# TensorE's code for each expert split in two parts, with all first parts placed behind the comparisons

## The chip, the cores and the metric

The kernel runs on one core of one Trainium2 chip. The metric is the time of one execution on the device, in microseconds (us). The trace comes from one profiled execution of the kernel before. Engines are named PE (TensorE matmuls), PEld (TensorE weight loads), DVE (VectorE), ACT (ScalarE), POOL (GpSimd) and SP (SyncE, which here only issues transfers).

## The reference, cut to what matters

Two layers of an encoder trunk on 256 tokens of width 1024, in float32. The change touches only the last block, a top-2-of-8 mixture of experts. Each token goes to two experts; an expert is a SwiGLU of inner width 3584:

```python
def swiglu(u, wg, wu, wd):
    return (jax.nn.silu(u @ wg) * (u @ wu)) @ wd

logits = (t @ w_router).astype(jnp.float32) + b_router.astype(jnp.float32)
top_val, top_idx = lax.top_k(logits, TOP_K)
gates = jax.nn.softmax(top_val, axis=-1)
# every expert e: swiglu of its own tokens with w_gate_e[e], w_up_e[e], w_down_e[e]
# y[token] += gate * output, for both experts of the token
```

How many tokens an expert gets is known only when the program runs.

## The kernel before, in words

After the mixer layers and the dense block, the tokens are sorted by expert into `xs`. The eight experts then run one after the other. POOL copies the tokens of the next expert into `xe` (which lies in `mixT`), and signals `xe_ready`.

The inner width is cut into 14 stages of 256 columns. A stage has three units of 1 MB: two halves of gate and up weights ("gu", s, 0) and ("gu", s, 1), each with 4 of the 8 slices of the input width, and one unit of down weights. SP streams the 42 units of each expert in order into 14 slots; a slot is refilled when the product that read it has signalled (`last_use` in the SP program: `gu_full` for gate and up, `down_done` for down). So the transfers run up to 14 units ahead, and past the end of an expert into the next.

PE, ACT and DVE each hold the code of an expert in six variants, for at most 32, 64, 128, 160, 192 and 256 tokens. `experts` (line 631) writes the code of one engine: the block "next" counts the expert up, "pick" loads its number of tokens into a register, and the chain beginning at "tree" compares it with the bounds, one comparison to a bound, and jumps to the variant. The chain ends in `first_variant`, whose code lies right behind it; the other variants follow in order of size. For all three engines that is 128. Each variant ends in a jump to "next", announced by a hint at the variant's beginning (`mark_branch_hint_location`).

PE's variants, with the lines of the profile:

- 32 and 64 tokens (`expert_whole`, line 1359): gate and up as full float32 products with the tokens as the stationary side (L1370), each run as two matmuls and two weight loads: 64 matmuls in a stage for 32 tokens, 32 for 64 tokens. Then the turned activations (L1356) and the down product (L1382). The order is gate_up(0); gate_up(1), turn(0); gate_up(2), turn(1), down(0); and so on. gate_up(2) and turn(0) wait for `act_ready`, which DVE gives (L2374) behind ACT's silu.
- 160 and 192 (`expert_wide`, line 1401): stage 0 runs in full float32 over four banks, PG and TRB (`gate_up_whole`, L1411, 64 matmuls, the first 32 from unit 0). All later stages use weights and tokens split into two float32r parts (L1427 and L1433 gate and up, L1446 and L1455 down). ACT makes the upper part of a unit (an activation, shown at L1575) and DVE the lower (L2380). With `HI` = 3 buffers for upper parts, ACT's second conversion waits for `hi_used`, which PE signals in the products of unit 0. DVE takes the tokens apart (L2407, and L2413 in two halves, the first behind `hi_used`), then empties the banks of stage 0 (L2427); the second stage on PE waits for that.
- 128 and 256 (`expert_split`, line 1482): split products in all stages (L1492 gate and up, L1523 down), so that the first product waits for ACT's first conversion.

In this run the experts 0 to 7 take the variants 32, 32, 128, 64, 160, 32, 192 and 64.

The order of the beginning of an expert on PE before the change is one piece of code:

```python
def expert(e, n):
    pe.wait_ge(xe_ready, e + 1)
    (expert_whole if n < P else expert_split if n % P == 0 else expert_wide)(e, n)
```

Of the kernel before, what the change touches and what calls it, by code (L numbers as in the profile page):

```python
# [24 lines left out]
P = 128  # L25
# [19 lines left out]
EARLY = SLOTS - D // SW  # L45
USES = 3 * STAGES
# [242 lines left out]
def build(nc, ap, out, ypairs):  # L289
# [13 lines left out]
    with ExitStack() as ctx:  # L303
# [327 lines left out]
        def experts(eng, name, emit, first_variant=128):  # L631
# [19 lines left out]
            for at, n, then in zip([label("tree")] + after, tests, after):  # L651
                with nc.body(at, valid_engines=own):
                    if n < first_variant:
                        eng.br_lt(rows, n + 1, on_true=label(n), on_false=then)
                    else:
                        eng.br_lt(rows, NVAR[NVAR.index(n) - 1] + 1, on_true=then, on_false=label(n))
            for n in sorted(NVAR, key=lambda n: n != first_variant):
                with nc.body(label(n), valid_engines=own):
# [136 lines left out]
        def _(pe):  # L795
# [563 lines left out]
            def expert_whole(e, n):  # L1359
# [26 lines left out]
                for i in range(STAGES + 2):  # L1386
                    if i < STAGES:
                        gate_up(i)
                    if 1 <= i <= STAGES:
# [11 lines left out]
            def expert_wide(e, n):  # L1401
# [3 lines left out]
                def gate_up_whole():  # L1405

                    for h in range(2):
                        w = landed_unit(e, "gu", 0, h).rearrange("p (k g f c) -> p k f g c", k=KD // 2, g=2, f=2)
                        for i, bank in enumerate(banks):
                            for k in range(KD // 2):  # L1410
                                last = mm(bank[:, 0:n], w[:, k, i // 2, i % 2, :], xe[:, h * KD // 2 + k, 0:n],  # L1411
                                          start=(h == 0 and k == 0), stop=(h == 1 and k == KD // 2 - 1))
                            if i == 2:
                                used = last
                        (used if h else last).then_inc(hi_used, 1)
                    last.then_inc(gu_full, 2)
# [52 lines left out]
                gate_up_whole()  # L1469
# [12 lines left out]
            def expert_split(e, n):  # L1482
# [57 lines left out]

                for s in range(STAGES + 1):
                    if s < STAGES:
# [7 lines left out]
            def expert(e, n):  # L1550
                pe.wait_ge(xe_ready, e + 1)
                (expert_whole if n < P else expert_split if n % P == 0 else expert_wide)(e, n)

            experts(pe, "pe", expert)
# [1068 lines left out]
```

## Time and profile before

| | |
|---|---|
| median of 3 runs | 1706.28 us (1705.0 to 1706.72) |
| the profiled execution, its own time | 1703.9 us |
| its span in the trace | 1702.1 us |
| PE busy | 1511.3 us, 89% of the span |
| PEld, DVE, ACT, POOL busy | 1199.1, 723.3, 552.1, 63.1 us |
| chain that ended last | PE 79%, DMA 11%, issue 4%, DVE 3% |
| granted TensorE clock, mean | 0.955 of full speed |
| the eight experts | from about 706 to 1675 us of the span |

"Issue" is time in which an engine waited for nothing that the profile shows: no semaphore of another engine came late. Behind such a wait can stand a transfer, the engine's own sequencer, or the loading of its code. In the rows of a timeline the columns are start (us), length (us), engine, line, operation, out<-in with shapes, count, and in brackets the idle time of the engine just before and what ended it. For a matmul the first shape is the stationary side. The clock in tenths or as a fraction is of full speed: 1.0 is 2.4 GHz and 0.5 is 1.2 GHz.

### The profile page before, as it was taken

How to read it: one execution, taken by the hardware profiler on the slowest of the kernel's cores; microseconds unless marked ns; L12 is line 12 of the kernel's file. 1: busy time of each engine (PE TensorE's matmuls, PEld its weight loads, DVE VectorE, ACT ScalarE, POOL GpSimd, SP SyncE). 2: the span in 40 equal slices, each digit the busy share in tenths (PEclk: the TensorE clock that was granted, in tenths of full speed). 3: DMA queues.
4: the chain of work that ended last, by engine and by line, in shares of the span. 5: the costliest groups of instructions: out<-in, count | busy, mean ns of one | idle time of the engine just before them, and what ended most of it. 6: DMA issues, size and time to landing. Idle time of an engine off the chain costs nothing.

```text
span 1702.1 us, 29831 instructions
## 1 busy us (share of the span) xinstructions
PE 1511.3 (89%) x12054; PEld 1199.1 (70%) x12055; DVE 723.3 (42%) x1056; ACT 552.1 (32%) x769; POOL 63.1 (4%) x66
## 2 busy tenths in 40 slices
PE   5999999999999999865658999999997579999894
PEld 3867878999976776644546875579986468888452
DVE  2253265656534532400017881156762036665212
ACT  2134144444322421200007761046551025554101
POOL 0010000000010001000000000000000000000002
PEclk9999999999999999987788999999999889999998
DMA  9725566545442435699999999997577997555893
GB/s 352 276 92 238 205 249 272 198 173 198 159 168 99 174 149 221 273 423 423 425 425 426 416 391 401 426 422 291 235 284 304 424 423 289 223 223 223 318 425 149
DMA packets 74557, 488.85 MB, mean 287 GB/s; under 512 B 9792, under 2 KB 13920, under 8 KB 16544
## 3 DMA queue, kind: packets, MB, share of 16 engines
q1 hardware_dynamic: 72176, 479.94, 70.2%
q10 hardware_dynamic: 1648, 4.59, 0.8%
q8 instruction: 114, 1.87, 0.4%
q0 software_dynamic: 576, 2.10, 0.4%
q14 instruction: 43, 0.35, 0.1%
HBM read 482.66 MB, written 3.93 MB: 286 GB/s over the span
## 4 chain that ended last, share of the span: by engine, by line
PE 79%; DMA 11%; issue 4%; DVE 3%; ACT 1%; POOL 1%; SPq 1%; ACTq 0%; POOLq 0%; DVEq 0%
PE PG L1370 9%; PE PG L923 6%; PE Y L949 5%; DMA arena<-in_experts 5%; PE PG L1492 5%; PE PG L1427 4%; PE Y L1382 4%; PE Y L1455 4%; DMA ring<-in_experts 4%; PE TRB L1427 4%; PE Y L1211 3%; PE Y L957 3%; PE PG L925 3%; PE TRB L1433 3%; PE PG L1433 3%
## 5 line engine op out<-in xcount | busy, mean ns | idle before, releaser
L1370 PE MATMUL PG<-ring,mixT 128*32 128x128 f32 (+1 forms) x1920 | 119.8, 356 | 60.7 <-issue 56.1
L2396 DVE COPY arena<-TRB 128x64 f32<-128x64 f32 (+1 forms) x70 | 17.6, 251 | 340.7 <-PE TRB L1356 340.7
L1370 PEld LDWEIGHTS PG<-ring,mixT 128*32 128x32 f32 (+1 forms) x1920 | 92.0, 140 | 91.3 <-issue 76.6
L1575 ACT ACTIVATE parts<-ring 128x2048 fp32r<-128x2048 f32 x82 | 153.6, 1901 | 3.6 <-PE PG L1492 3.6
L923 PE MATMUL PG<-h_parts,parts 128*128 128x512 f32 x432 | 152.8, 394 | 1.4 <-DVE arena L2275 1.4
L1575 ACT ACTIVATE rope<-PG 64x128 f32<-64x128 f32 (+2 forms) x84 | 27.1, 323 | 377.5 <-PE PG L1370 353.9
L1370 PE MATMUL PG<-arena,mixT 128*32 128x128 f32 (+1 forms) x1664 | 101.8, 351 | 41.0 <-issue 41.0
L1370 PEld LDWEIGHTS PG<-arena,mixT 128*32 128x32 f32 (+1 forms) x1664 | 78.9, 139 | 68.8 <-issue 55.2
L925 PE MATMUL PG<-h_parts,parts 128*128 128x256 f32 x432 | 121.8, 282 | 0.0
L2260 DVE TENSOR_TENSOR parts<-ring,parts 128x2048 fp32r<-128x2048 f32 x42 | 95.1, 2290 | 32.7 <-ACT parts L1575 32.7
L2380 DVE TENSOR_TENSOR ring_parts<-ring,parts 128x2048 fp32r<-128x2048 f32 x40 | 90.6, 2288 | 31.7 <-PE Y L1446 16.3
L2380 DVE TENSOR_TENSOR parts<-arena,parts 128x2048 fp32r<-128x2048 f32 x42 | 95.2, 2288 | 17.7 <-PE Y L1446 15.1
L923 PEld LDWEIGHTS PG<-h_parts,parts 128*128 128x128 f32 x432 | 81.2, 188 | 19.4 <-DVE arena L2275 1.6
L949 PE MATMUL Y<-hT,ring 128*128 128x256 f32 x416 | 93.2, 384 | 0.0
L949 PEld LDWEIGHTS Y<-hT,ring 128*128 128x128 f32 x416 | 79.5, 193 | 11.5 <-issue 0.8
L925 PEld LDWEIGHTS PG<-h_parts,parts 128*128 128x128 f32 x432 | 81.3, 188 | 0.0
L1575 ACT ACTIVATE parts<-arena 128x2048 fp32r<-128x2048 f32 x42 | 78.9, 1901 | 3.6 <-PE PG L1492 3.6
L890 PE MATMUL Y<-parts 128*128 128x256 f32 x224 | 63.4, 283 | 0.2 <-DVE parts L2284 0.2
L892 PE MATMUL Y<-parts 128*128 128x256 f32 x224 | 63.4, 283 | 0.0
L891 PE MATMUL Y<-parts 128*128 128x256 f32 x224 | 63.4, 283 | 0.0
L957 PE MATMUL Y<-ring,hT 128*128 128x256 f32 (+2 forms) x320 | 57.3, 338 | 2.8 <-ACT hT L1575 2.8
L2380 DVE TENSOR_TENSOR parts<-arena,scr_parts 128x2048 fp32r<-128x2048 f32 x21 | 48.1, 2293 | 26.4 <-ACT scr_parts L1575 26.4
(364 smaller groups left out, 2675.1 us busy)
## 6 DMA issues: line engine op xcount, KB each, us to landing
ring<-in_experts SPq DMA_DIRECT2D x168, 1024.0 KB, 13.6
arena<-in_experts SPq DMA_DIRECT2D x168, 1024.0 KB, 16.9
ring<-in_weights SPq DMA_DIRECT2D x116, 1024.0 KB, 6.4
ring<-in_weights SPq DMA_DIRECT2D x4, 512.0 KB, 4.1
ypairs<-hT ACTq DMA_DIRECT2D x3, 512.0 KB, 6.6
tok<-in_x SPq DMA_DIRECT2D x1, 1024.0 KB, 9.0
result<-scr SPq DMA_DIRECT2D x2, 512.0 KB, 2.6
ring<-in_weights SPq DMA_DIRECT2D x2, 432.0 KB, 6.3
```

Of the source, the lines that this page charges most:

```text
L923: mm(PG[:, m, :].rearrange("p (i t) -> p i t", i=2), w_hi[d % SPLITS][:, c], h_parts[:, :, k, :], start=(k == 0), stop=False, skip_group_c ...
L925: last = mm(PG[:, m, 0:T], w_lo[d % SPLITS][:, c], h_hi[:, k, :], start=False, stop=(k == KD - 1), skip_group_check=True)
L949: last = mm(bank_part, ring[:, s, k, c:c + m], hT[:, k, :], start=(k == 0), stop=(k == KD - 1))
L957: last = mm(bank_part, hT[:, k, b * P:(b + 1) * P], ring[:, s, k, 0:m], start=(k == 0), stop=(k == KD - 1))
L1370: last = mm(bank[i * n:(i + 1) * n, 0:width], xe[:, k, 0:n], w[k // 4][:, k % 4, i * width:(i + 1) * width], start=(k == 0), stop=(k == KD ...
L1382: last = mm(o, actT[:, s % 2, f, 0:n], w[:, f, c:c + width], start=(s == 0 and f == 0), stop=(s == STAGES - 1 and f == 1))
L1427: last = mm(both, hi[:, k, i // 2, i % 2, :], h_parts[:, :, h * KD // 2 + k, 0:n], start=(h == 0 and k == 0), stop=False, skip_group_check ...
L1433: last = mm(bank[:, 0:n], lo[:, k, i // 2, i % 2, :], h_parts[:, 0, h * KD // 2 + k, 0:n], start=False, stop=(h == 1 and k == KD // 2 - 1) ...
L1492: last = mm(bank, x[j][:, h * KD // 2 + k, :], w[:, k, :], start=(opens and k == 0), stop=(closes and k == KD // 2 - 1))
L1575: return nc.scalar.activation(out_, in_, func, **kw)
L2260: V.tensor_tensor(w_lo[d % SPLITS], ring[:, slot_of[slot_of_dense(d)], :, :].rearrange("p k c -> p (k c)"), w_hi[d % SPLITS].bitcast(F32), ...
L2380: V.tensor_tensor(w_lo_e[q % SLOTS_E], ring_e[q % SLOTS_E].rearrange("p k c -> p (k c)"), w_hi_e[q % HI].bitcast(F32), ALU.subtract).then_ ...
```

## The change

PE's variants alone are cut in two. The first part ("head") has the wait for `xe_ready` and the first products: gate_up(0) for 32, 64, 128 and 256 tokens, and the half of stage 0 that reads unit 0 for 160 and 192. All six heads stand right behind the comparisons, in the order of `HEADS`; then come the rests, that of 64 first and then 32, 128, 160, 192, 256. A head ends in a jump to its rest, with a hint at the head's beginning. The chain of comparisons of PE now ends in 64 instead of 128. The products, their order in a variant and all semaphores stay; ACT's and DVE's code stays.

```diff
+HEADS = (64, 192, 160, 128, 32, 256)
...
-        def experts(eng, name, emit, first_variant=128):
+        def experts(eng, name, emit, first_variant=128, heads=None):
...
+            if heads:
+                for n in HEADS:
+                    with nc.body(label(n), valid_engines=own):
+                        on = eng.mark_branch_hint_location()
+                        heads(eng.snap(turn, min_val=0, max_val=NE - 1), n)
+                        eng.br(label(f"rest_{n}")).branch_hint(on)
             for n in sorted(NVAR, key=lambda n: n != first_variant):
-                with nc.body(label(n), valid_engines=own):
+                with nc.body(label(f"rest_{n}" if heads else n), valid_engines=own):
                     back = eng.mark_branch_hint_location()
                     emit(eng.snap(turn, min_val=0, max_val=NE - 1), n)
                     eng.br(label("next")).branch_hint(back)
...
-            def expert_whole(e, n):
+            def expert_whole(e, n, head):
...
-                for i in range(STAGES + 2):
+                if head:
+                    gate_up(0)
+                    return
+                for i in range(1, STAGES + 2):
...
-            def expert_wide(e, n):
+            def expert_wide(e, n, head):
...
-                gate_up_whole()
+                if head:
+                    gate_up_whole(0)
+                    return
+                gate_up_whole(1)
...
-            def expert_split(e, n):
+            def expert_split(e, n, head):
...
+                if head:
+                    gate_up(0)
+                    return
                 for s in range(STAGES + 1):
-                    if s < STAGES:
+                    if 0 < s < STAGES:
                         gate_up(s)
...
-            def expert(e, n):
+            def part(e, n, head):
+                (expert_whole if n < P else expert_split if n % P == 0 else expert_wide)(e, n, head)
+
+            def expert_head(e, n):
                 pe.wait_ge(xe_ready, e + 1)
-                (expert_whole if n < P else expert_split if n % P == 0 else expert_wide)(e, n)
-
-            experts(pe, "pe", expert)
+                part(e, n, True)
+
+            def expert_rest(e, n):
+                part(e, n, False)
+
+            experts(pe, "pe", expert_rest, first_variant=HEADS[0], heads=expert_head)
```

## Rows read from the trace of the kernel before

**Rows 1.** Windows: experts 1, 3 and 6; length, busy (x count), PEclk, DMA share, GB/s.

```profile
785.00:891.00 106.00, 65.50 (x1148) 49.58 (x1148) 8.47 (x32) 6.14 (x19) 1.90 (x1) 0.77 1.01 424
...
1023.00:1110.00 87.00, 84.47 (x619) 47.73 (x617) 10.77 (x29) 7.13 (x16) 1.90 (x1) 1.00 1.01 414
...
1375.00:1583.00 208.00, 198.79 (x1175) 169.92 (x1176) 122.23 (x101) 100.16 (x98) 1.90 (x1) 0.98 0.67 269
```

**Rows 2.** DMA queues, 784 to 797.5 us: packets, MB, share of 16 engines.

```profile
q8 instruction: 3, 0.05, 1.7%
```

**Rows 3.** Timeline of PE, start of expert 1 (32 tokens, behind an expert of 32).

```profile
791.54 2.79 PE L1370 MATMUL PG<-ring,mixT 128*32 128x128 f32 x48 [6.88 <-issue]
796.77 3.70 PE L1370 MATMUL PG<-ring,mixT 128*32 128x128 f32 x80 [2.44 <-issue]
```

**Rows 4.** Timeline of PE, start of expert 2 (128 tokens).

```profile
897.27 3.77 PE L1492 MATMUL PG<-scr_parts,h_parts 128*128 128x512 f32 x8 [6.98 <-ACT scr_parts L1575]
```

**Rows 5.** Timeline of PE, start of expert 3 (64 tokens, behind 128).

```profile
1023.50 2.38 PE L1370 MATMUL PG<-ring,mixT 128*64 128x256 f32 x20
1027.64 4.97 PE L1370 MATMUL PG<-ring,mixT 128*64 128x256 f32 x44 [1.76 <-issue]
```

**Rows 6.** Chain that ended last, before stage 13 of expert 3.

```profile
1098.95 0.77 issue
```

**Rows 7.** Timeline of PE, start of expert 4 (160 tokens, behind 64).

```profile
1110.05 2.17 PE L1411 MATMUL PG<-mixT,ring 128*128 128x160 f32 x14
1114.81 0.67 PE L1411 MATMUL PG<-mixT,ring 128*128 128x160 f32 x2 [2.59 <-issue]
1115.27 3.93 PE L1411 MATMUL TRB<-mixT,ring 128*128 128x160 f32 x16
...
1124.70 1.44 PE L1427 MATMUL PG<-h_parts,parts 128*128 128x320 f32 x8 [1.15 <-DVE rope L2427]
```

**Rows 8.** Timeline of PE, start of expert 0 (32 tokens).

```profile
706.29 4.95 PE L1370 MATMUL PG<-ring,mixT 128*32 128x128 f32 x128 [4.54 <-POOL mixT L2588]
```

**Rows 9.** Timeline of PE, start of expert 5 (32 tokens, behind 160).

```profile
1294.64 6.12 PE L1370 MATMUL PG<-ring,mixT 128*32 128x128 f32 x128 [5.44 <-issue]
```

**Rows 10.** Timeline of PE, start of expert 6 (192 tokens, behind 32).

```profile
1381.89 4.25 PE L1411 MATMUL PG<-mixT,ring 128*128 128x192 f32 x16 [6.92 <-issue]
1385.98 2.76 PE L1411 MATMUL TRB<-mixT,ring 128*128 128x192 f32 x16
...
1395.23 1.67 PE L1427 MATMUL PG<-h_parts,parts 128*128 128x384 f32 x8 [1.29 <-DVE rope L2427]
```

**Rows 11.** Timeline of ACT, start of expert 6.

```profile
1376.87 0.38 ACTq L1895 DMA_DIRECT2D ypairs<-hT  x1
1383.95 1.28 ACT L1575 ACT_TABLE_LOAD   x1 [8.01 <-issue]
...
1388.78 1.91 ACT L1575 ACTIVATE scr_parts<-ring 128x2048 fp32r<-128x2048 f32 x1 [1.62 <-PE TRB L1411]
```

**Rows 12.** Timeline of DVE, start of expert 6.

```profile
1387.19 2.29 DVE L2380 TENSOR_TENSOR ring_parts<-ring,parts 128x2048 fp32r<-128x2048 f32 x1 [9.17 <-ACT parts L1575]
...
1390.72 2.29 DVE L2380 TENSOR_TENSOR ring_parts<-ring,scr_parts 128x2048 fp32r<-128x2048 f32 x1 [0.37 <-ACT scr_parts L1575]
...
1393.98 0.56 DVE L2427 COPY rope<-PG 128x384 f32<-128x384 f32 x1 [0.96 <-PE TRB L1411]
```

**Rows 13.** Timeline of PE, start of expert 7 (64 tokens, behind 192).

```profile
1589.66 8.74 PE L1370 MATMUL PG<-ring,mixT 128*64 128x256 f32 x64 [6.11 <-issue]
1598.32 0.71 PE L1356 MATMUL TRB<-con,rope 64*128 64x128 f32 x4
```

**Rows 14.** Timeline of ACT, start of expert 7.

```profile
1585.97 1.14 ACTq L1895 DMA_DIRECT2D ypairs<-hT  x2
1595.02 1.28 ACT L1575 ACT_TABLE_LOAD   x1 [10.23 <-PE PG L1370]
1596.32 0.38 ACT L1575 ACTIVATE rope<-PG 64x256 f32<-64x256 f32 x1
```

## Prediction before the run

> **What bounds the kernel now.** I read the busy time of each engine by expert first, to see what limits each; then PE's timeline at the eight starts; then the chain that ended last; then ACT and DVE at the starts where PE is not alone.
>
> In experts 0 and 1 the 16 DMA engines are full while PE works 62% of the time at a mean clock of 0.77; in expert 6 the DMA share is 0.67 and PE is busy 199 of 208 us [rows 1]. So the 32-token experts (0, 1, 5) run at the pace of their 42 MB, and the 128, 160 and 192 experts (2, 4, 6) at PE's. Expert 3 (64 tokens) uses up the lead of the ring: before its stage 13 PE waits 0.77 us on "issue" in the chain [rows 6], with the DMA share at 1.01 [rows 1], which I read as a late transfer. Between the 32- and 64-token starts PE's idle time is of another kind. It waits 6.88 us "for issue" ahead of expert 1 and again 2.44 us after 48 matmuls [rows 3], 5.44, 6.92 and 6.11 us ahead of experts 5, 6 and 7 [rows 9, 10, 13], and three packets of the instruction queue, 0.05 MB in all, pass around the first [rows 2]. That is code being loaded. Experts 3 and 4 begin without a wait but stop after 20 and 14 matmuls [rows 5, 7].
>
> **How code arrives.** The stops tell where blocks of code end. Variant 32 begins about 101 instructions before a block's end (48 matmuls, their loads, four others), 64 about 45, 160 about 32. Variant 32 has 2 x 1,148 instructions of matmuls and loads [rows 1] and by my estimate 64 others; 101 - 2,360 and 45 differ by 2,304, nine times 256, so a block holds 256 instructions, and 0.05 MB over three packets is 64 bytes an instruction. PE asks for the following block when it enters one. In expert 1 the second block is usable 5.2 us after the first (791.54 to 796.77 [rows 3]); across the jumps the wait is 5.4 to 6.9 us. I take 5 us from request to use, between the nearest ends of 4 and 6.4 us.
> "next" and the comparisons cost nothing that shows: expert 3 starts at once behind five blocks of the 128 variant [rows 5]. The Trainium skill (Runtime: NRT & Kernel Launch, section Instruction fetch mechanics) says that a taken branch outside the current two-block window must wait for a fetch. The trace disagrees for a target announced by a hint, as "next" is [rows 5]; by the page's rule the new jump to every rest would wait in full, which is the third rival.
>
> **The change part by part.** Removed: nothing; every product stays. Added per expert: one hint and one jump, 0 to 0.2 us each for 8 experts by the invisible cost of today's comparisons [rows 5]; I take 0, since PE's sequencer runs ahead of its matmuls. Moved: code. Variant 128, today right ahead of 32 and by my count 1,152 instructions long, begins 27 instructions into a block, and there the first head will begin. By counting (heads of about 69, 68, 68, 58, 133 and 110) the heads of 64, 192 and 160 fit in the block of "next", 128 straddles its end and 32 lies in the second block; rest 64 and rest 192 then begin some 235 instructions before a block's end, but rest 32 about 29 and rest 160 about 26. These two stop again after 14 matmuls. The counts may be off by ten.
>
> Expert 0. The head waits for POOL until 706.3 as now [rows 8], with its rest already loaded. Then rest 32 stops for the second block: gate_up(1), done now at 711.2, would be done at about 715.5. It releases units 2 and 3 for refill. The ring's stream begins with stage 0's release, two units of 2.5 us each (1 MB at 424 GB/s [rows 1]), which hide most of the 4 us. Loss 0.4 us (0 to 2).
>
> Expert 1: transfers bound it, with the DMA share at 1.01 while PE stops for 9 us at its start [rows 1, 3]. 0. Expert 2: PE waits for ACT's first conversion until 897.27 [rows 4]; the fetches fit in those 7 us. 0.
>
> Expert 3: the head's 32 matmuls run from 1023.5 to 1027.0 at 0.108 us each (20 take 2.38 [rows 5]). The hint is met some 1.5 us before the head's first matmul, so the rest is usable at about 1027.2 instead of 1027.64 with 12 matmuls still to do. gate_up(1) ends at about 1031.1 instead of 1032.6: gain 1.4 (0 to 1.76). It passes on: the refill is released earlier by the same, and expert 3 ends on the transfers [rows 6].
>
> Expert 4: the stop of 2.59 us [rows 7] moves from instruction 32 to the end of rest 160's first block, about as long, with the same half clock behind it. But the wait before the second stage is already DVE's, 1.15 us [rows 7]. Gain 0.2 (-1.5 to 0.8).
>
> Expert 5: the head is in the second block, which is asked for on entering "next" and so, by my estimate, usable 1.7 us (0 to 3) before the 1294.64 of now [rows 9]; stage 0's release starts the refill 2 us earlier, but gate_up(1) is done 2 to 5 us later. Gain 0.3 (-2 to 2).
>
> Expert 6, where most seems to lie: PE could start 6.4 us earlier, at 1375.5, half a microsecond behind the last down product (1381.89 - 6.92 [rows 10]). Yet the second stage waits for DVE [rows 10], DVE for ACT's first conversion, and that for ACT's own code: ACT issues its last transfer at 1376.87 and shows nothing until 1383.95 [rows 11]. What PE's earlier products can remove is DVE's 0.37 and 0.96 us of idle time [rows 12]: 1.3 us. Against it PE now idles 6 to 7 us before the second stage. After the 6.92 us of idle time the first 16 matmuls took 4.25 us, the next 16 2.76 [rows 10]: I read that as the granted clock at its lower level (1.2 GHz), 1.5 us lost. A second such stretch, ahead of a stage that sets the path, gives 1.3 - 1.7: loss 0.4 (-1.7 to 1.3).
>
> Expert 7: no conversion stands before it. The head runs from 1584.1 to 1587.6, the rest is usable 5 us after the hint at about 1583.9, so at 1589, and gate_up(1) ends before 1594.4 even at half clock. Then turn(0) waits for ACT, whose code comes late here too. From its last transfer (1585.97 + 1.14 [rows 14]) its code takes between nothing, the lower end, and 6.7 us as before expert 6 [rows 11]; the place is like that one, so I take a value near the upper end, 5.8: 1592.9. With the table load, the silu and the gate, 1.28 + 0.38 + 0.5 us [rows 14], turn(0) starts at 1595.1 instead of 1598.32 [rows 13]: gain 3.2 (2.0 to 3.8). It reaches the end, since transfers and products of this expert shift together.
>
> Sum: -0.4 + 1.4 + 0.2 + 0.3 - 0.4 + 3.2 = 4.3 us. Against the profiled execution, 1703.9 (span 1702.1 and 1.8 around it), that is 1699.6; the median of the runs is 2.4 higher, so 1706.28 - 4.3 = 1702.0. What is late next is ACT's code, in experts 6 and 7.
>
> **The rivals.**
> First, more gain: rest 32 and rest 160 do not end a block so soon (the counts are off by more than 25), and PE's clock holds in expert 6. Then experts 0 and 4 give 0 and 0.8, 5 gives 2, 3 gives 1.7, 6 gives 1.2 and 7 3.8: 9.5, so 1696.8. For it: my count of the other instructions is an estimate. Against: three stops agree with it. 15%.
> Second, the other side: the second fetch after the head costs its upper price of 6.4 us. It decides once it is later than the head's own saving: experts 0, 4 and 5 lose 2, 2 and 2.5, while 3, 6 and 7 give 1.4, -0.5 and 3.2: net loss 2.4, so 1708.7, and up to 1711 with expert 3's gain gone and a full clock loss. For it: in expert 1 both fetches were slow while the transfers ran at 424 GB/s [rows 1, 3]. 25%.
> Third, the hint does not cover: the jump to a rest waits 5 us after the head. Expert 3 loses 4, since its variant no longer lies in a block already there; 4 loses 5, 5 3, 0 5, and 7 still gains 1: about 1722. Against: the hint for "next" works eight times. 8%.
> Fourth, the change does nothing to the path, since other waits replace all of it: 1706. 5%.
>
> **How the numbers follow.** The forecast has 47%; its own range is 1699.5 to 1704. 0.2%, or 3.4 us, is about what a measurement can tell from no change. Of the forecast 9% stay inside it. Faster: 38 + 15 = 53%. Same: 9 + 17 of the second rival + 5 = 31%. Slower: 8 of the second and 8 of the third, 16%. The range 1697.5 to 1709.5 leaves out the third rival and the ends of the first two.
>
> **What would show it.** In the timeline of PE: expert 6 and 7 start within 1 us of the last down product; expert 7's turn(0) comes about 11.5 us behind the end of expert 6 instead of 14.8, with ACT ahead of it; expert 6's second stage starts as late as before within 1.3 us, behind DVE, at half clock. In 32- and 160-token experts a second stop follows about 14 matmuls into gate_up(1) or the second half. Stops between head and rest of 5 us, or second stops that delay the full DMA stream after expert 0, would make it wrong.

## The result and the profile after

The changed kernel takes 1719.38 us (median of 5 runs, 1717.32 to 1723.28), the kernel before 1706.72 beside it: ratio 1.0072, 95% interval 1.0059 to 1.0084. It is slower by 12.7 us where I forecast 4.3 faster. The profiled execution took 1718.58, with a span of 1716.8 us, 14.7 longer than before. The mean granted clock is 0.948 (before 0.955), and "issue" is 6% of the chain that ended last (before 4%). One execution of run 14, 1761.12 us at a mean clock of 0.879, fell into a slower state of the chip and is left out of its median.

The timeline of PE, kernel after, at the starts of the eight experts but expert 2:

```profile
708.43 3.64 PE L1377 MATMUL PG<-ring,mixT 128*32 128x128 f32 x64 [4.54 <-POOL mixT L2610]
712.37 1.39 PE L1377 MATMUL PG<-ring,mixT 128*32 128x128 f32 x19 [0.30 <-issue]
715.45 1.51 PE L1377 MATMUL PG<-ring,mixT 128*32 128x128 f32 x45 [1.69 <-issue]
...
793.32 3.64 PE L1377 MATMUL PG<-ring,mixT 128*32 128x128 f32 x64 [6.55 <-issue]
801.98 1.46 PE L1377 MATMUL PG<-ring,mixT 128*32 128x128 f32 x19 [5.02 <-issue]
807.53 2.78 PE L1377 MATMUL PG<-ring,mixT 128*32 128x128 f32 x45 [4.09 <-issue]
...
1036.60 5.94 PE L1377 MATMUL PG<-ring,mixT 128*64 128x256 f32 x32 [5.14 <-issue]
1042.47 0.71 PE L1363 MATMUL TRB<-con,rope 64*128 64x128 f32 x4
...
1127.20 2.03 PE L1420 MATMUL TRB<-mixT,ring 128*128 128x160 f32 x13 [1.01 <-issue]
1132.80 2.02 PE L1437 MATMUL PG<-h_parts,parts 128*128 128x320 f32 x8 [3.56 <-DVE rope L2449]
...
1307.20 3.64 PE L1377 MATMUL PG<-ring,mixT 128*32 128x128 f32 x64 [8.35 <-issue]
1313.12 0.81 PE L1377 MATMUL PG<-ring,mixT 128*32 128x128 f32 x19 [2.27 <-issue]
1318.53 2.75 PE L1377 MATMUL PG<-ring,mixT 128*32 128x128 f32 x45 [4.60 <-issue]
1321.21 0.48 PE L1363 MATMUL TRB<-con,rope 64*128 64x128 f32 x2
...
1393.19 2.86 PE L1420 MATMUL PG<-mixT,ring 128*128 128x192 f32 x16 [0.83 <-issue]
1401.99 4.49 PE L1420 MATMUL PG<-mixT,ring 128*128 128x192 f32 x16 [3.34 <-issue]
1411.31 1.67 PE L1437 MATMUL PG<-h_parts,parts 128*128 128x384 f32 x8 [2.17 <-DVE rope L2449]
...
1600.77 3.67 PE L1377 MATMUL PG<-ring,mixT 128*64 128x256 f32 x32 [1.18 <-issue]
1607.20 5.36 PE L1377 MATMUL PG<-ring,mixT 128*64 128x256 f32 x32 [2.76 <-issue]
1612.49 0.71 PE L1363 MATMUL TRB<-con,rope 64*128 64x128 f32 x4
```

What to see. In each expert the first group is the head and the second begins the rest. The brackets of the second groups are what is left of the jump: 5.02, 5.14, 2.27, 3.34 and 2.76 us, and in expert 0, where the head waits for POOL, 0.30. The 32-token experts stop a second time after 19 products (1.69, 4.09, 4.60). The early starts did come in experts 6 and 7, with idle times of 0.83 and 1.18 us where there were 6.92 and 6.11 [rows 10, 13].

The same places on both time axes (us from the start of each span; the last column is an experiment, explained below, that changes only where the code lies):

| place | before | after | difference | after with pads |
|---|---|---|---|---|
| expert 0, first product | 706.29 | 708.43 | +2.1 | 706.21 |
| expert 1, first product | 791.54 | 793.32 | +1.8 | 792.06 |
| expert 2, first product | 897.27 | 901.38 | +4.1 | 900.31 |
| expert 3, first product | 1023.50 | 1027.78 | +4.3 | 1026.46 |
| expert 3, turn(0) | 1032.54 | 1042.47 | +9.9 | 1035.08 |
| expert 4, first product | 1110.05 | 1118.99 | +8.9 | 1111.60 |
| expert 5, first product | 1294.64 | 1307.20 | +12.6 | 1296.54 |
| expert 5, turn(0) | 1300.72 | 1321.21 | +20.5 | 1306.14 |
| expert 6, second stage | 1395.23 | 1411.31 | +16.1 | 1396.27 |
| expert 7, turn(0) | 1598.32 | 1612.49 | +14.2 | 1597.67 |

The first 2.1 us are older than the change's first instruction: of them 1.3 are a wait for a weight transfer in the first 100 us, 4.5 us in two waits in this execution and 3.2 in that of before. That is about as much as the profiles lie further apart (14.7) than the medians (12.7). What belongs to the change comes in two places: expert 3 (+5.6 up to its turn(0), of which it gives back 1.0), and experts 4 to 5 (+3.7 up to expert 5's first product, and +3.5 more when expert 6 reaches its second stage). Expert 6's body and expert 7's start give 1.9 back. Another 2.3 us appear in expert 1, seen at expert 2, but they are not shown to be the change's: run 12, in which PE's code is that of before, takes 108.4 us from expert 1's first product to expert 2's, the changed kernel 108.1 and the kernel before 105.7.

The lower clock follows the stops. In expert 7, 32 products behind the stop of 2.76 us take 5.36 us at a mean granted clock of 0.68, and as many ahead of it 3.67 at 1.00. ("At half clock" below means that a group begins at the lower level; the mean over the group lies between the levels.) Over expert 3 the granted clock is 0.96 instead of 1.00, and the DMA share 0.95 instead of 1.01 [rows 1]: the transfers are no longer at their limit. The window of expert 3, kernel after (length, busy and count of PE, PEld, DVE, ACT, POOL, PEclk, DMA share, GB/s):

```profile
1026.00:1113.00 87.00, 81.86 (x599) 46.58 (x599) 9.76 (x26) 7.15 (x16) 0.49 (x1) 0.96 0.95 389
```

### The profile page after: what moved, and what is told of

Its sections match the earlier page's. It is cut to its first block, busy times and chain, and to the rows that moved or that the text cites. A ratio compares the mean times of both kernels' runs of the same rounds, so it can differ in the third digit from the quotient of the medians.

```text
span 1716.8 us, 29858 instructions
## 1 busy us (share of the span) xinstructions
PE 1512.5 (88%) x12054; PEld 1196.4 (70%) x12055; DVE 723.4 (42%) x1056; ACT 552.4 (32%) x769; POOL 63.2 (4%) x66
## 4 chain that ended last, share of the span: by engine, by line
PE 79%; DMA 8%; issue 6%; DVE 3%; ACT 2%; SPq 1%; POOL 1%; ACTq 0%; POOLq 0%; DVEq 0%
PE PG L1377 10%; PE PG L930 6%; PE Y L956 5%; PE PG L1505 5%; PE Y L1389 5%; PE PG L1437 4%; PE Y L1465 4%; PE TRB L1437 4%; PE Y L964 3%; PE Y L1218 3%; DMA arena<-in_experts 3%; PE PG L932 3%; DMA ring<-in_experts 3%; PE TRB L1443 3%; PE PG L1443 3%
```

## The experiments

The line numbers in a row are those of the kernel that it comes from.

**1. The changed kernel, without the hint ahead of the jump.**

```diff
-                        on = eng.mark_branch_hint_location()
                         heads(eng.snap(turn, min_val=0, max_val=NE - 1), n)
-                        eng.br(label(f"rest_{n}")).branch_hint(on)
+                        eng.br(label(f"rest_{n}"))
```

> The changed kernel without the new hint at a head's beginning; the jump to the rest stays. Theory A (the hint does not start a fetch, the jump does): the same time as the changed kernel, 1719 us within 3 us, and the gaps of PE between head and rest stay: 5.0 us in expert 1, 5.1 in expert 3, 3.3 in expert 6, 2.8 in expert 7. Theory B (the hint starts the fetch, but behind that of the following block): each of these gaps grows by 1 to 3 us, and the time by 4 to 8 us, to 1723 to 1727.

Measured: 1723.6 us, ratio to before 1.0100 (1.0083 to 1.0117), so some 4 us slower than with the hint. PE at expert 3, this kernel:

```profile
1043.26 5.05 PE L1376 MATMUL PG<-ring,mixT 128*64 128x256 f32 x28 [6.24 <-issue]
```

The stop between head and rest is 6.24 us without the hint and 5.14 with it; in expert 1 5.2 and 5.0, in expert 5 2.7 and 2.3, in experts 6 and 7 3.0 and 3.4 against 3.3 and 2.8. So a hint set ahead of a head's products, which take 3.6 us, gives about 0 to 1 us. The time is in theory B's range, while the stops grow by less than it asked for. Only in expert 0, where the head first waits for POOL, does it do its work: the stop is 2.2 us without and 0.3 with it.

**2. The kernel before, without the hint at the beginning of PE's variants.**

```diff
-                    back = eng.mark_branch_hint_location()
+                    hinted = name != "pe"
+                    if hinted:
+                        back = eng.mark_branch_hint_location()
...
-                    eng.br(label("next")).branch_hint(back)
+                    jump = eng.br(label("next"))
+                    if hinted:
+                        jump.branch_hint(back)
```

> The kernel before, with PE's old hint for the jump back to the next expert taken out (ACT and DVE keep theirs). Theory A (hints do nothing for PE, what is loaded stays because several blocks are held): same time as before, 1706 us within 2, and experts 3 and 4 still start without a gap. Theory B (this hint is what holds or loads the block of the comparisons): every start of an expert waits about 5 us more, which counts in experts 3, 4, 5 and 7: 15 to 20 us slower, 1721 to 1726.

Measured: 1722.97 us, ratio 1.0099 (1.0082 to 1.0116). PE at experts 1, 4 and 6, this kernel:

```profile
798.17 2.95 PE L1374 MATMUL PG<-ring,mixT 128*32 128x128 f32 x49 [12.64 <-issue]
...
1116.65 3.56 PE L1415 MATMUL PG<-mixT,ring 128*128 128x160 f32 x12 [4.73 <-issue]
...
1396.07 4.42 PE L1415 MATMUL PG<-mixT,ring 128*128 128x192 f32 x16 [12.78 <-issue]
```

The starts that took 6.88, 0 and 6.92 us [rows 3, 7, 10] take 12.64, 4.73 and 12.78, those of experts 5 and 7 8.85 and 9.93 instead of 5.44 and 6.11 [rows 9, 13]: these jumps wait 3.4 to 5.9 us more for their target. So the old hint is worth 16 us in all. Expert 3 is the exception, this kernel:

```profile
1027.20 7.13 PE L1374 MATMUL PG<-ring,mixT 128*64 128x256 f32 x64
```

It starts at once without any hint, so PE still held the block of "next", by the prediction's count five blocks back. And its second stop is gone, 1.76 us before [rows 5]; so is expert 4's, 2.59 us before [rows 7]. The early hint has a price, then: I read that it takes the place of the request for the following block, which is the block that these stops wait for. Late in expert 2 the instruction queue fits that: here it moves a block at 1009.0 us, and in the kernel before none between 979.5 and 1025.0 us.

The Trainium skill (Runtime: NRT & Kernel Launch, section Instruction fetch mechanics) says that a taken branch outside the current two-block window must wait for a fetch. The trace agrees at experts 1, 4, 5, 6 and 7, by the times above; it does not at expert 3, where the measurement decides.

**3. The kernel before, with PE's variant of 64 tokens first and no heads** (`experts(pe, "pe", expert, first_variant=64)`): the change of order alone.

> The kernel before, without heads, with only the order of PE's variants changed: the chain of comparisons ends in 64 instead of 128, so that the whole variant for 64 tokens lies right behind it. If what counts is whether the variant's first block is already loaded, experts 3 and 7 start within 1 us and have no second stop: 1.8 us gained in expert 3, 3 to 4 in expert 7, none lost elsewhere, 1701 us. If the loss of the changed kernel comes from the new order rather than from the cut, this kernel is slower than before by 3 us or more.

Measured: 1707.62 us, ratio 1.0004 (0.9992 to 1.0015): no difference. Its trace shows two that cancel. PE at experts 1, 6 and 7, then ACT at expert 7, this kernel:

```profile
793.97 6.47 PE L1370 MATMUL PG<-ring,mixT 128*32 128x128 f32 x128 [10.87 <-issue]
...
1383.79 4.33 PE L1411 MATMUL PG<-mixT,ring 128*128 128x192 f32 x16 [10.97 <-issue]
...
1586.66 7.13 PE L1370 MATMUL PG<-ring,mixT 128*64 128x256 f32 x64 [1.12 <-issue]
1598.65 1.22 PE L1356 MATMUL TRB<-con,rope 64*128 64x128 f32 x4 [4.86 <-DVE rope L2374]
```

```profile
1596.39 1.28 ACT L1575 ACT_TABLE_LOAD   x1 [9.60 <-issue]
```

Expert 7 starts after 1.12 us instead of 6.11 and its 64 products run at full clock. Then PE idles 4.86 us for DVE, which waits for ACT, which has issued nothing for 9.60 us. And experts 1 and 6 wait 4 us longer for their start than before (10.87 and 10.97 us); run 10 looks into that.

**4. The changed kernel with the rests in the old order** (that of 128 first; the comparisons still end in the head of 64, and `HEADS` is as in the change).

> The changed kernel with the rests in the old order (128 first, then 32, 64, 160, 192, 256). Rest 64 lies right behind rest 32 again and its first block may still be loaded from expert 1. If the 5.1 us gap in expert 3 comes from the new order, it is gone here and the time falls by 4 to 5 us, to 1714.5. If the jump from head to rest costs a fetch in any order, expert 3 keeps its gap of about 5 us and the time stays at 1719 within 3.

Measured: 1712.68 us, ratio 1.0042 (1.0026 to 1.0059). Expert 3's stop is gone and so are the second stops of experts 1 and 5; the stops between head and rest stay. PE at expert 1, this kernel:

```profile
796.18 3.48 PE L1377 MATMUL PG<-ring,mixT 128*32 128x128 f32 x64 [10.77 <-issue]
804.73 3.64 PE L1377 MATMUL PG<-ring,mixT 128*32 128x128 f32 x64 [5.08 <-issue]
```

So heads cost some 6 us in this order, and the new order of the rests another 7.

**5. The kernel before, with the hint of the 32- and 64-token variants late**: it is set within the last gate and up product of the variant instead of at its beginning, by my count in the same block of code as the jump.

```diff
                     for k in range(KD):
+                        if k == (4 if n == 32 else 1):
+                            late = pe.mark_branch_hint_location()
...
-                    emit(eng.snap(turn, min_val=0, max_val=NE - 1), n)
-                    eng.br(label("next")).branch_hint(back)
+                    late = emit(eng.snap(turn, min_val=0, max_val=NE - 1), n)
+                    eng.br(label("next")).branch_hint(late or back)
```

> The kernel before with the hint for the jump to the next expert moved, in the 32- and 64-token variants alone, from the variant's beginning into its last gate and up product, more than 5 us ahead of the jump but inside the variant's last block of code. Theory C (a hint takes effect when the engine enters the block that holds the jump, in place of the request for the following block; one that is met later in that block is served only at the jump): the starts of experts 1, 2, 4 and 6 wait 5 us more, as without a hint; on the path these count in experts 4 and partly elsewhere: 5 to 9 us slower, 1712 to 1716. Theory B (a hint starts its fetch at once, 5 us suffice): same time as before, 1706.5 within 2.

Measured: 1712.33 us (9 runs), ratio 1.0029 (1.0017 to 1.0040). The starts are not late: expert 1 waits 6.78 us, expert 4 starts at once and expert 6 waits 7.12, as with the early hint. So a hint this late does the same work; that it starts its fetch at once is not shown. Expert 4's second stop is gone, as without a hint (run 2), while expert 3's, behind the 128 variant with its early hint, stays (1.44 us). Why this kernel is slower all the same is not settled. 1.4 us of it are in expert 4, which takes 185.96 us up to expert 5's first product instead of 184.59: behind 5.08 us of idle time for DVE its second stage runs at half clock (2.50 us instead of 1.44 for the same 8 products [rows 7]), although it starts 0.6 us sooner after the expert's first product.

**6 and 7. Pads of additions.** The changed kernel, and the kernel of run 3, each with blocks of register additions that never run between PE's variants, meant to shift the code behind them by 45 to 211 instructions. The second stop moved by one product only, so the shift was about 2 instructions: I take it that each row of additions was folded into one. These two runs are near repeats of the changed kernel and of run 3, and what was expected of them was not tried.

> The changed kernel with instructions that are never run put between the rests, so that rest 32 begins early in a block and ends late in one, and rest 160 ends late in one. Theory C: the second stop in the 32-token experts (4.1 us in expert 1, 4.6 in expert 5) and the 3.4 us of the late return before expert 5 are gone, 1 us less in expert 4; the stops between head and rest stay (5.1 us in expert 3, 2.8 in expert 7). Time 1709 to 1712. If the losses of the changed kernel lie in the jumps alone, it stays at 1717 to 1720.

Measured: 1718.48 us, ratio 1.0065 (1.0049 to 1.0082), with the second stops where they were, 18 products into the rest (3.74 us in expert 1).

> The kernel before without heads, variant 64 first, and 115 instructions that are never run ahead of variant 32, so that it ends late in a block as in the kernel before. Theory C: the late returns of 4.3 us that the same order had without them, before experts 1, 2 and 6, are gone, and the gain of expert 3 stays: 1702 to 1705. If offsets in a block do not matter, 1707.6 as without them.

Measured: 1707.40 us, ratio 0.9996 (0.9982 to 1.0009).

**8. Run 7 with the variant of 64 tokens first on ACT and DVE too** (`first_variant=64` for all three).

> The kernel of the run before this one, with variant 64 right behind the comparisons on ACT and DVE too. If expert 7 is held up by ACT's code, its first turned activations come right behind gate_up(1), 8 to 9 us after expert 6's last product instead of 13 to 15; expert 2 begins up to 5 us later, since ACT's variant 128 is no longer there at once. Time 1700 to 1706. If ACT's code is no bound, expert 7 is unchanged and the time is 1 to 5 us longer.

Measured: 1699.16 us, ratio 0.9958 (0.9941 to 0.9974): 8 us faster than run 7. PE and then ACT at expert 7, this kernel:

```profile
1584.94 7.13 PE L1380 MATMUL PG<-ring,mixT 128*64 128x256 f32 x64 [1.11 <-issue]
1592.00 0.71 PE L1366 MATMUL TRB<-con,rope 64*128 64x128 f32 x4
```

```profile
1589.29 1.28 ACT L1585 ACT_TABLE_LOAD   x1 [4.21 <-PE PG L1380]
```

ACT is now released by PE's product and not by its own code, and turn(0) follows the products without a gap: 7.06 us after the first product, where run 3 has 11.99.

**9. The changed kernel with pads that stay.** Products that never run, of four instructions each, ahead of the rests: 11, 53, 48 and 16 of them for 32, 128, 160 and 192 tokens. The jump to them hangs on a comparison that is never met.

```diff
+                if name == "pe" and n in PADS:
+                    with nc.body(label(f"pad_{n}"), valid_engines=own):
+                        for _ in range(PADS[n]):
+                            nc.tensor.matmul(tr[0][:, 0:P], ident, ident, start=True, stop=True)
+                        later = [m for m in PADS if list(PADS).index(m) > list(PADS).index(n)]
+                        eng.br(label(f"pad_{later[0]}" if later else "done"))
```

> The changed kernel, with matrix products that never run (11, 53, 48 and 16 products of four instructions each) ahead of the rests of 32, 128, 160 and 192 tokens, so that every rest begins about 240 instructions ahead of the end of a block of code. Theory (a second stop stands where the block ends): the stops after 19 products of a 32-token rest (1.7, 4.1 and 4.6 us in experts 0, 1 and 5) are gone from their place, and come after more than 100 products and shorter than 2 us, or not at all; the stop between head and rest stays at 2 to 5 us. Time 1714 to 1717.5 us. Rival (the second stop follows the hinted jump itself, since the next request is delayed): the stops stay after 19 products, time 1719 us.

Measured: 1704.17 us (10 runs), ratio 0.9984 (0.9972 to 0.9996): 15 us faster than the changed kernel, by positions alone, and far below both expectations. PE at experts 1, 3 and 5, this kernel:

```profile
800.54 3.64 PE L1387 MATMUL PG<-ring,mixT 128*32 128x128 f32 x64 [4.85 <-issue]
804.11 0.48 PE L1373 MATMUL TRB<-con,rope 64*128 64x128 f32 x2
...
1031.47 3.67 PE L1387 MATMUL PG<-ring,mixT 128*64 128x256 f32 x32 [1.34 <-issue]
1035.08 0.71 PE L1373 MATMUL TRB<-con,rope 64*128 64x128 f32 x4
...
1296.54 3.64 PE L1387 MATMUL PG<-ring,mixT 128*32 128x128 f32 x64 [3.68 <-issue]
1302.83 3.38 PE L1387 MATMUL PG<-ring,mixT 128*32 128x128 f32 x64 [2.65 <-issue]
```

The second stops are gone from the 19th product, as the theory had it. Two things come on top: expert 3's stop is 1.34 us instead of 5.14, although its own code did not move, and expert 5 starts after 3.68 us instead of 8.35. The instruction queue says what became of the first. (I take q8 as PE's: its packets are 16 KB, one block of 256 instructions.) The DMA queues of the stretch from "next" to the first products of expert 3's rest, in the changed kernel (1024 to 1038 us) and here (1023 to 1034 us):

```profile
q8 instruction: 2, 0.03, 0.8%
```

```profile
q8 instruction: 1, 0.02, 0.5%
```

Two blocks are fetched before the rest runs on in the changed kernel, and one in this. In slices of half a microsecond the two lie at 1028.0 and 1033.5 us and the rest begins at 1036.60; the one lies at 1028.5 and the rest begins at 1031.47. So the rest follows the last of them by 3 us in both, and the second block, which comes 5.5 us behind the first, covers the 3.8 us between the stops. I read the first of the two as the block behind "next", asked for ahead of the hint, and the second as the hint's own; which blocks they are the queue does not say.

**10. Run 8 with a pad that stays**: 28 products ahead of PE's variant of 32 tokens, 112 instructions.

> The kernel before with the variant of 64 tokens first on PE, ACT and DVE, and 28 products that never run (112 instructions) between PE's variants of 64 and 32 tokens, so that variant 32 ends some 100 instructions later in its last block. Theory (the request for the next block at the entry of the last one stands before the hinted block): the idle time ahead of experts 1, 2 and 6 falls by 3 to 4 us, from 8.4, 7.4 and 9.1; but expert 1 is bound by transfers and 2 and 6 by ACT's conversion, so the time gains 0 to 1.5 us: 1697.7 to 1699.5. Rival (PE's start sets the path there): 1692 to 1695.

Measured: 1701.30 us (7 runs), ratio 0.9962 (0.9949 to 0.9976); run 8's interval covers it. The idle time ahead of experts 1 and 6 falls from 8.37 and 9.09 us to 6.95 and 7.44, less than half of what I expected, and the time does not fall, as it should not by the theory that transfers and ACT's conversion set the path there; it lies above that theory's range of 1697.7 to 1699.5. By my count variant 32 ends about 100 instructions into its last block in run 8 and 210 in this run, so that the request made on entering that block is further along when the jump comes. That this is the whole cause is not shown: run 3, whose code lies two instructions from run 8's, waits 10.87 and 10.97 us, and run 7, whose code on PE is that of run 8, 10.91 and 8.76.

**11. The changed kernel with ACT's and DVE's variants of 64 tokens first.**

> The changed kernel with ACT's and DVE's variants of 64 tokens first too. Theory (in expert 7 the changed kernel's turn(0) follows its products at half clock and not ACT): the time stays within 2 us of the changed kernel, 1717.5 to 1719.5. Rival (ACT's code still bounds expert 7 in the changed kernel): 1712 to 1715, as it gave 8 us to the kernel before with PE's variant 64 first.

Measured: 1714.42 us (7 runs), ratio 1.0040 (1.0025 to 1.0054). That lies between the two expectations. The profiled execution, 1718.42, is the slowest of the seven; its span of 1716.6 us is 0.2 from the changed kernel's, but its parts differ. It reaches expert 2 3.2 us later after expert 0's first product (196.1 us against 192.9), and in expert 7 turn(0) comes 9.90 us behind the first product instead of 11.72. There it still follows PE's products without a gap, so PE and not ACT sets it, as the theory had it; but the 32 products behind the stop run at full clock, 3.67 us instead of 5.36. Why the clock held here, and what makes the runs faster, is not settled.

**12. The kernel before with only ACT's and DVE's variants of 64 tokens first.**

> The kernel before with only ACT's and DVE's variants of 64 tokens first; PE stays as before. Theory (in expert 7 PE's own start and ACT's code end together, so that neither alone gives much): PE's start stays at 6 us after the last product of expert 6 and turn(0) follows gate_up(1) by less than 1 us; gain 0.5 to 2.5 us: 1704 to 1706. Rival 1 (ACT's code sets turn(0) alone, as the prediction had it): turn(0) 5 us earlier, 1700 to 1701. Rival 2 (ACT's variant 128, no longer right behind the comparisons, costs as much in expert 2): 1707 to 1709.

Measured: 1707.11 us (12 runs), ratio 0.9996 (0.9985 to 1.0007): nothing. PE at expert 7, this kernel:

```profile
1592.39 9.56 PE L1370 MATMUL PG<-ring,mixT 128*64 128x256 f32 x64 [5.48 <-issue]
```

So PE's late start and ACT's late code cover each other in expert 7. From expert 6's second stage to expert 7's turn(0) the traces have 203.1 us before, 201.4 in run 3, 203.3 in run 12 and 196.5 in run 8: there mending PE alone gives 1.7 us, ACT and DVE alone nothing, and all three 6.6. Over the whole kernel it is nothing, nothing and 8 us.

**13. The changed kernel with one pad of exactly one block**, 64 products (256 instructions) ahead of the rest of 32.

> The changed kernel with 64 products that never run (256 instructions, one block of code) ahead of the rest of 32 tokens: every later rest keeps its place inside its block, and lies one block further. Theory A (what counts is the place inside a block, where a stretch ends and the next block is needed): nothing changes, the second stops of 4 us after 19 products and expert 3's stop of 5 us stay, 1717.5 to 1720.5 us. Theory B (expert 3 depends on which of the blocks behind the comparisons are still there, and so on a block's number): expert 3's stop between head and rest falls to 1.3 us as with the four pads, the second stops stay, 1710 to 1715 us.

Measured: 1720.19 us (4 runs), ratio 1.0081 (1.0064 to 1.0099), and expert 3's stop is 5.53 us, the second stop in expert 5 4.68. A shift by one block changes nothing that can be told from the scatter.

**14. The changed kernel with one pad of 44 instructions** (11 products) ahead of the rest of 32.

> The changed kernel with 11 products that never run (44 instructions) ahead of the rest of 32 tokens: the rest of 32 now begins 16 instructions into a block, and the rests of 128, 160 and 192 tokens 44 instructions later than in the changed kernel. Theory A (the place inside a block): the second stops of experts 0, 1 and 5 are gone; expert 4, whose rest now begins early in a block too, loses its second stop of 1 us; expert 3's stop may stay at 5 us or go, as variant 128 ends 44 instructions later in its block. 1706 to 1714 us, by how expert 3 goes. Theory B: expert 3's stop stays for certain, since no block's number changes by one for most of the code: 1711 to 1714.

Measured: 1711.82 us (5 runs), ratio 1.0031 (1.0017 to 1.0044). The second stops are gone, and expert 5 starts after 3.79 us. Expert 3 stops as long as before, but elsewhere, this kernel:

```profile
1031.25 5.93 PE L1387 MATMUL PG<-ring,mixT 128*64 128x256 f32 x32 [5.44 <-issue]
1037.66 3.67 PE L1387 MATMUL PG<-ring,mixT 128*64 128x256 f32 x32 [0.48 <-issue]
```

The stop now stands ahead of the head, on the way through "next", and between head and rest only 0.48 us are left. So 44 instructions in the right place give 7 of the 15 us, and the other three pads the rest of them.

Runs 9 and 13 together narrow down expert 3's stop. By count both shift the rest of 128 tokens, which runs just ahead of it, by about 256 instructions, and neither moves expert 3's own code; they differ ahead of expert 3 only in where the rest of 32 lies. Yet the stop is 1.34 us in one and 5.53 in the other. So it hangs on where the code of experts 0 and 1 lay, which ran 130 us and more before; how is open.

**15. Run 9 with ACT's and DVE's variants of 64 tokens first.**

> The changed kernel with the four pads, and ACT's and DVE's variants of 64 tokens first. With the pads alone turn(0) of expert 7 came 12.0 us after PE's first product there, with 3.0 us between head and rest and half clock behind it. Theory (PE's stop between head and rest bounds expert 7): gain 0 to 1.7 us against the pads alone, 1702.5 to 1704.2. Rival (ACT's code bounds it): 1698 to 1700, as with variant 64 first on all three engines and no split.

Measured: 1700.41 us (7 runs), ratio 0.9966 (0.9954 to 0.9979). PE at expert 7, this kernel:

```profile
1591.78 5.36 PE L1387 MATMUL PG<-ring,mixT 128*64 128x256 f32 x32 [2.73 <-issue]
1597.07 0.71 PE L1373 MATMUL TRB<-con,rope 64*128 64x128 f32 x4
```

In the trace PE's own stop and the half clock behind it still set turn(0), 11.7 us after the first product (run 8: 7.06); the span, 1701.3, is 0.7 below run 9's. The runs lie lower than that, between the two expectations.

Four kernels beat both the kernel before and the changed one: run 8 (0.9958), run 10 (0.9962) and run 15 (0.9966), whose intervals overlap, and by less run 9 (0.9984). The simplest has no heads at all, and names 64 as the first variant on three engines.

## Why the prediction was wrong, step by step

**The step that failed first** is "the hint is met some 1.5 us before the head's first matmul, so the rest is usable" 5 us after it. That time from request to use was about right for one request. But I let the hint's request stand alone. The runs show two packets of the queue ahead of expert 3's rest, 5.5 us apart, against one in run 9; stops of 5.02 and 5.14 us where I had 0 and a gain; and almost the same stop without any hint (run 1). My reading is that PE, on entering "next", asks for the block behind it, and that the hint's block comes only after that. The evidence that I leaned on, "the hint for 'next' works eight times", was for a hint set long before its jump, and at one of the eight, expert 3, none was needed (run 2). Run 5 shows that a late one can work too, so lateness alone is not what costs; that an open request is, fits the packets but was not tried by itself.

Two smaller slips of the working: 20 products in 2.38 us are 0.119 us each and not 0.108 (32 took 3.67), and the half clock in expert 6, read as 1.5 us, went into the sum as 1.7.

**Expert 1: "transfers bound it: 0"** is neither borne out nor refuted. The trace has +2.3 us behind 5.02 and 4.09 us of stops, and with the pads, which take away the second of them, still +2.5 (3.0 at expert 2, 0.5 at expert 1). A later release of the first units could do that. But run 12, with PE's code of before, has +2.7, so that the stretch scatters by as much.

**Expert 3: "gain 1.4"** turned into a loss of 5.6 up to turn(0). I had seen that its variant would lie elsewhere only in the third rival. With the pads the expert takes 85.14 us from its first product to that of expert 4, against 86.55 before: a gain of 1.4, the number of the prediction, but in part by luck. I had all of it at the end of gate_up(1); there it is 0.4 (turn(0) 8.62 us behind the first product instead of 9.04), and the rest comes later, where the wait of 0.77 us before stage 13 [rows 6] is absent. The head does shorten the start; the changed kernel's positions hide it.

**Expert 4: the second stop** was to move "about as long". It is 1.01 us instead of 2.59, but ahead of the second stage PE waits 3.56 us for DVE instead of 1.15 [rows 7]. Up to that stage expert 4 gains 0.8 us, the upper end of my range; it loses it again through the second stage at half clock (2.02 us instead of 1.44 for the same 8 products) and the late start of expert 5.

**Expert 5: "gain 0.3 (-2 to 2)"** was the largest miss. The start was to be 1.7 us earlier and comes 2.9 later (8.35 against 5.44): a term that I did not have. I counted where rests begin, never where they end, and read it as how far into its last block of code the variant before ends. Runs 9 and 14 give that start back with a shift alone (3.68, 3.79), so that it is a matter of position is shown; which position is not. Behind it come the stops of 2.27 and 4.60; I had them at "2 to 5 us later", and they are 7.9 at turn(0), of which 4.4 are made good by expert 6's second stage.

**The count of the second stop** was 14 products and is 19: the estimate was off by 10 instructions, within its margin. That there would be such a stop was right (runs 9 and 14 take it away).

**Expert 6: "loss 0.4"**, measured between expert 5's stop and the second stage, cannot be told apart from the recovery there. The reading of it was right in kind: PE starts 0.83 us behind the last product and waits for DVE all the same, 2.17 us instead of 1.29, with 3.34 us of idle time and half clock on the way.

**Expert 7: "gain 3.2 (2.0 to 3.8)"** was 1.9, from 14.2 to 16.1 in the table. ACT's code came as I took it: 5.26 us from the end of its last transfer to its table load, and I had 5.8. ACT at expert 7, kernel after:

```profile
1602.00 1.14 ACTq L1917 DMA_DIRECT2D ypairs<-hT  x2
1608.40 1.28 ACT L1597 ACT_TABLE_LOAD   x1 [7.58 <-issue]
```

What set turn(0) was PE, through the stop and the half clock behind it: 5.36 us instead of 3.67 for 32 products. I had allowed for half clock and taken it as covered.

**The rivals.** The third, at 8%, "the hint does not cover: about 1722", is the one that came, 2.6 us from the result. Its terms were 4, 5, 3 and 5 us in experts 3, 4, 5 and 0; the path shows 5.6, nothing, 3.7 and later 3.5, and nothing in expert 0, with 2.3 in expert 1 that may be scatter, so its total is close in part by luck. I priced it as a hint that fails altogether and gave it little for that reason. That a hint may come in second was no case of mine, although the trace of before had a sign: two blocks for one start, one after the other, 5.2 us apart [rows 3]. The second rival, at 25%, priced a dear second fetch at 6.4 us; the second stops were 1.69, 4.09 and 4.60, and the result lies 8 us beyond its end of 1711.

**What stays open.** Which blocks PE still holds when it comes back to "next": in run 14 the start of expert 3 waits where it did not in the other kernels, and runs 9 and 13 differ there though the code next to it is shifted alike. And why run 5 is slower, and why most runs of 11 and 15 lie below the profiled ones.

## What to carry to other kernels

A jump to code that is not there cost 3.4 to 5.9 us here (run 2), and a hint ahead of 3.6 us of products did not cover it: give a hint more time than that, and keep what runs first and what follows it in one piece of code. Before code is cut or reordered, count both where each piece begins in its 256-instruction block and where it ends; here 44 instructions of padding were worth 7 us, and four pads 15, more than the idea itself (about 3 us faster than the kernel before, run 9). Where several engines jump at the same place, mend them together: PE alone and ACT with DVE alone gave nothing, all three 8 us.

## What the runs showed of the hardware that I had not expected

- A hint ahead of 3.6 us of products gave about 0 to 1 us, where two blocks came 5.5 us apart ahead of its target (runs 1 and 9); a hint in the last gate and up product of a variant gave all of it (run 5: 6.78 us ahead of expert 1, against 6.88 [rows 3] and 12.64 without a hint).
- An early hint cost as well as gave: without it the second stops of experts 3 and 4, 1.76 and 2.59 us, are gone (run 2).
- PE can come back to code that it ran several blocks before without a wait: expert 3 starts at once behind the 128 variant without any hint (run 2), and in run 3 with the 64 variant right behind "next". The changed kernel, whose heads lie between, stops 5.14 us.
- The place of code inside its block of 256 instructions matters: a shift by one block gave 1720.19 us against 1719.38, a shift by 44 instructions 1711.82.
